# The first gate chunk of a feed-forward stage, computed before its shift is known

## The reference, cut to what matters

```python
mod = jax.nn.silu(c) @ ada_w + ada_b
sh1, sc1, g1, sh2, sc2, g2, sh3, sc3, g3 = jnp.split(mod, 9, axis=-1)
u = x * (1 + sc1[:, None, :]) + sh1[:, None, :]
y = (jax.nn.silu(u @ w_gate) * (u @ w_up)) @ w_down
x = layer_norm(ALPHA * x + 0.5 * (1 + g1[:, None, :]) * y, ln1_g, ln1_b)
...
```

## Time and profile before

| | |
|---|---|
| time, median of 3 runs | 1893.94 us (1893.53 to 1897.15) |
| span of the profiled execution | 1887.7 us (its own time beside the span is not listed; the median of the runs lies 6.2 us above the span) |
| TensorE busy | 1821.9 us, 97% of the span |
| VectorE, ScalarE, GpSimd busy | 1064.9, 817.2, 498.3 us |
| mean granted TensorE clock | 0.988 of full speed |
| chain that ended last | PE 76%, DVE 7%, POOL 7%, ACT 3%, issue 3%, DMA 3% |

### The profile page before, as it was taken

How to read it: one execution, slowest core, us unless ns; L and a number is a source line. 1 busy time by engine, 2 the same in 40 slices (tenths; PEclk the granted TensorE clock), 3 DMA queues, 4 the chain that set the end, 5 groups by cost and what they waited for, 6 DMA issues and landing times.

```text
span 1887.7 us, 22977 instructions
## 1 busy us (share of the span) xinstructions
PE 1821.9 (97%) x8904; PEld 1488.6 (79%) x8904; DVE 1064.9 (56%) x1092; ACT 817.2 (43%) x864; POOL 498.3 (26%) x644
## 2 busy tenths in 40 slices
PE   4999999999999998999999999988999999999998
PEld 3888888877887677887888888867998867888877
DVE  6565657567888896546323333368652445656452
ACT  3222223247666856227433432275222547333351
POOL 0411111032999481001000000050104996211100
PEclk8999999999999999999999999999999999999999
DMA  8566656553243133443332323354733321552411
GB/s 319 166 190 182 193 174 196 159 188 122 89 132 136 55 123 134 137 154 101 102 99 89 104 68 93 106 165 173 154 93 125 120 94 38 178 176 92 145 45 45
DMA packets 204213, 247.82 MB, mean 131 GB/s; under 512 B 5899, under 2 KB 184875, under 8 KB 202091
## 3 DMA queue, kind: packets, MB, share of 16 engines
q1 hardware_dynamic: 185643, 171.27, 28.5%
q0 software_dynamic: 13472, 51.42, 9.8%
q10 hardware_dynamic: 5024, 24.12, 3.4%
HBM read 227.39 MB, written 19.40 MB: 131 GB/s over the span
## 4 chain that ended last, share of the span: by engine, by line
PE 76%; DVE 7%; POOL 7%; ACT 3%; issue 3%; DMA 3%; SPq 1%; POOLq 0%; DVEq 0%; ACTq 0%
PE ps L2328 24%; PE ps L2131 20%; PE ps L2197 11%; POOL conv_out L488 6%; PE ps L2161 4%; PE ps L2508 2%; PE ps L2663 2%; DVE w_lo L1229 2%; PE ps L2581 2%; ACT w_hi L605 1%; DMA s_in<-u_scratch 1%; PE ps L2496 1%; DMA w_raw<-in_ffn_w_gate 1%; PE ps L2517 1%; PE ps L2563 1%
## 5 line engine op out<-in xcount | busy, mean ns | idle before, releaser
L1229 DVE TENSOR_TENSOR w_lo<-w_raw,w_hi 128x2048 fp32r<-128x2048 f32 x158 | 369.6, 2339 | 503.4 <-ACT w_hi L605 501.2
L605 ACT ACTIVATE w_hi<-w_raw 128x2048 fp32r<-128x2048 f32 x156 | 298.4, 1913 | 639.1 <-PE ps L2328 232.4
L2131 PE MATMUL ps<-u_hi,w_hi 128*128 128x512 f32 x656 | 260.1, 397 | 10.5 <-DVE w_lo L1229 10.5
L2131 PE MATMUL ps<-u_lo,w_hi 128*128 128x512 f32 x656 | 256.9, 392 | 0.0
L2131 PE MATMUL ps<-u_hi,w_lo 128*128 128x512 f32 x656 | 256.5, 391 | 0.0
L2328 PE MATMUL ps<-u_hi,w_hi 128*128 128x512 f32 x656 | 256.3, 391 | 0.0
L2328 PE MATMUL ps<-u_hi,w_lo 128*128 128x512 f32 x656 | 255.4, 389 | 0.0
L2328 PE MATMUL ps<-u_lo,w_hi 128*128 128x512 f32 x656 | 255.3, 389 | 0.0
L488 POOL TENSOR_TENSOR conv_out<-conv_out,conv_tap 128x512 f32<-128x512 f32 x120 | 194.6, 1622 | 72.0 <-ACT conv_tap L786 55.2
L2131 PEld LDWEIGHTS ps<-u_hi,w_hi 128*128 128x128 f32 x656 | 124.3, 189 | 39.4 <-DVE w_lo L1229 8.3
L2131 PEld LDWEIGHTS ps<-u_lo,w_hi 128*128 128x128 f32 x656 | 124.4, 190 | 26.1 <-issue 0.7
(11 more groups left out here) (507 smaller groups left out, 3280.8 us busy)
## 6 DMA issues: line engine op xcount, KB each, us to landing
w_raw<-in_w_in SPq DMA_DIRECT2D x44, 1024.0 KB, 5.1
ada_raw<-in_ada_w POOLq DMA_DIRECT2D x56, 512.0 KB, 4.8
w_raw<-in_ffn_w_gate SPq DMA_DIRECT2D x22, 1024.0 KB, 5.4
w_raw<-in_ffn_w_up SPq DMA_DIRECT2D x22, 1024.0 KB, 5.3
w_raw<-in_ffn_w_down SPq DMA_DIRECT2D x32, 704.0 KB, 4.5
ada_first<-in_ada_w SPq DMA_DIRECT2D x8, 1024.0 KB, 14.5
w_raw<-in_w_out SPq DMA_DIRECT2D x8, 1024.0 KB, 5.1
w_raw<-in_xa_wk SPq DMA_DIRECT2D x4, 1024.0 KB, 5.3
```

The lines of the kernel that those rows point to most:

```text
L605: A(WHI[:, slot], WRAW[:, slot], ACT.Copy).then_inc(s["w_hi"], 1)
L1229: V.tensor_tensor(WLO[:, slot], WRAW[:, slot], WHI[:, slot].bitcast(F32), ALU.subtract).then_inc(s["w_lo"], 1)
L2131: ins = M(PS[:, 2 * j + t, 0:n], w[:, j, at_:at_ + P], a[:, k, 0:n], start=(k == 0 and q == 0), stop=(k == KT - 1 and q == 2))
```

## The change

Chunk 0 (gate) is computed on x times (1 + scale) alone. The product of the weights with the shift vector, one number for each of the 256 output columns, is made by 16 products of the raw float32 weights with one column (`shift_columns`) and added as the bias of the two Silu instructions. `UH` and `UL` first hold the scaled input and are overwritten with the scaled and shifted input when chunk 0 has been computed; chunk 1 (up) is computed on that as before. The input rows are loaded ahead of the scale slices, the gate chunk ahead of the shift slices. SP loads nothing of the next pair before the small products are done, as they read the raw weights. Six of the eight rests of the scaled input are made on POOL. `lo(1, 1)` is taken into `modulate_lo`, ahead of its third k tile.

```diff
+        VF = at("x_scaled", T0, [P, 4, L])
+        SHB = at("gate_shift", S0 + 7.75, [P, 2])
@@ SP
+            sp.dma_start(XN[:], I["x"][0].rearrange("(t p) d -> p t d", p=P)).then_inc(s["x_load"], 16)
             ada_slices(0)
-            sp.dma_start(XN[:], I["x"][0].rearrange("(t p) d -> p t d", p=P)).then_inc(s["x_load"], 16)
...
+                load(0, None, 0, wk8(wg)[:, :, 0:256], True)
                 ada_slices(1)
-                load(0, None, 0, wk8(wg)[:, :, 0:256], True)
                 load(1, None, 0, wk8(wu)[:, :, 0:256], True)
                 parameter_rows()
+                sp.wait_ge(s["bias_mm"], 1)
@@ POOL, ahead of the first ada_group
+            for f in range(2, KT):
+                pool.wait_ge(s["scaled"], 2 * f + 2)
+                nc.gpsimd.tensor_tensor(UL[:, f], VF[:, f % 4], UH[:, f].bitcast(F32), ALU.subtract).then_inc(s["vl_pool"], 1)
@@ ScalarE, in ffn_act: the first pair is taken out of the loop
+                if shifted:
+                    hi_step(ph, 0, 2, 0)
+                    act.wait_ge(s["mm"], 1)
+                    act.wait_ge(s["bias_ready"], 1)
+                    act.wait_ge(s["ul_ready"], KT)
+                    A(SIL[:, 0], PS[:, 0], ACT.Silu, bias=SHB[:, 0:1])
+                    A(SIL[:, 1], PS[:, 1], ACT.Silu, bias=SHB[:, 1:2]).then_inc(s["free0"], 1)
+                    hidden(0)
+                    parameter_copies()
...
             first_hi(0)
             act.wait_ge(s["modx_ready"], 1)
+            for f in range(KT):
+                act.wait_ge(s["x_ready"], f + 1)
+                A(UH[:, f], X[:, f], ACT.Copy, scale=MODX[:, f:f + 1]).then_inc(s["scaled"], 1)
+                if f >= 4:
+                    act.wait_ge(s["vl_dve"], 2)
+                    if f >= 6:
+                        act.wait_ge(s["vl_pool"], f - 5)
+                A(VF[:, f % 4], X[:, f], ACT.Copy, scale=MODX[:, f:f + 1]).then_inc(s["scaled"], 1)
+            first_hi(1)
             act.wait_ge(s["mod_ready"], 2)
+            act.wait_ge(s["mm"], 1)
             modulate_hi(0, lambda f: MODX[:, f:f + 1], lambda f: MOD[:, SH1 + f:SH1 + f + 1])
-            first_hi(1)
@@ VectorE
             ada_first_part(0)
+            lo(0, 0)
             mod_cols(8, 16, 8)
             dve.wait_ge(s["mod_ready"], 1)
             derived(0, SC1, False).then_inc(s["modx_ready"], 1)
+            for f in range(2):
+                dve.wait_ge(s["scaled"], 2 * f + 2)
+                V.tensor_tensor(UL[:, f], VF[:, f], UH[:, f].bitcast(F32), ALU.subtract).then_inc(s["vl_dve"], 1)
             ada_first_part(1)
-            lo(0, 0)
             mod_cols(0, 8, 16)
...
-            modulate_lo(0, lambda f: MODX[:, f:f + 1], lambda f: MOD[:, SH1 + f:SH1 + f + 1])
-            lo(1, 1)
+            dve.wait_ge(s["mm"], 1)
+            dve.wait_ge(s["vl_pool"], KT - 2)
+            modulate_lo(0, lambda f: MODX[:, f:f + 1], lambda f: MOD[:, SH1 + f:SH1 + f + 1], between=lambda: lo(1, 1))
+            dve.wait_ge(s["bias_mm"], 1)
+            V.tensor_copy(SHB[:], PS[:, 6, 0:2]).then_inc(s["bias_ready"], 1)
@@ TensorE: transposes of x now ahead of mod_first(0); then
+                def part(w, a, k, j=0):
+                    for t in range(2):
+                        at_ = 256 * k + P * t
+                        ins = M(PS[:, 2 * j + t], w[:, j, at_:at_ + P], a[:, k], ...)
+                    return ins
+                def unshifted_chunk():
+                    pe.wait_ge(s["w_lo"], CB[ph] + 1)
+                    pe.wait_ge(free[0], UB[ph])
+                    for k in range(KT):
+                        if k == 6:
+                            pe.wait_ge(s["mod_ready"], 1)
+                            mod_first(1)
+                        pe.wait_ge(s["scaled"], 2 * k + 1)
+                        part(WHI, UH, k)
+                        part(WLO, UH, k)
+                        pe.wait_ge(*((s["vl_pool"], k - 1) if k >= 2 else (s["vl_dve"], k + 1)))
+                        ins = part(WHI, UL, k)
+                    ins.then_inc(s["mm"], 1)
+                def shift_columns():
+                    pe.wait_ge(s["mod_ready"], 2)
+                    for t in range(2):
+                        for k in range(KT):
+                            at_ = 256 * k + P * t
+                            ins = M(PS[:, 6, t:t + 1], WRAW[:, 0, at_:at_ + P], MOD[:, SH1 + k:SH1 + k + 1],
+                                    start=(k == 0), stop=(k == KT - 1))
+                    ins.then_inc(s["bias_mm"], 1)
+                def second_chunk():
+                    pe.wait_ge(s["w_lo"], CB[ph] + 2)
+                    pe.wait_ge(free[1], UB[ph])
+                    for k in range(KT):
+                        pe.wait_ge(s["ul_ready"], n_ul + k + 1)
+                        part(WHI, UH, k, 1)
                        part(WLO, UH, k, 1)
                        ins = part(WHI, UL, k, 1)
                    ins.then_inc(s["mm"], 1)
...
-                    first_chunk()
+                    unshifted_chunk()
+                    shift_columns()
+                    second_chunk()
                     parameter_columns()
-                    chunk(0, 1)
```

More of the change, by code:

```diff
@@ L284, in build_program @@
                  "y_mm y_gelu y_store yf_load sgs_load yh2 yl2 gsig gz gzn zh zl mem_load "
-                 "mem_ss mem_root mem_scaled mem_t mf_ready mh ml kv_store kv_load s_mm smax_ready exp_done "
-                 "s_sum p_scaled p_t pt_ready o_mm oh ol xrow_ready row_sum row_ss or_ready out_store "
-                 "consts_load dec_load0 dec_load1 s5_ranged s5_pows").split()
+                 "mem_ss mem_scaled mf_ready mh ml kv_store kv_load s_mm smax_ready exp_done "
+                 "s_sum p_scaled pt_ready o_mm oh ol xrow_ready row_sum row_ss or_ready out_store "
+                 "consts_load dec_load0 dec_load1 s5_ranged s5_pows scaled vl_dve vl_pool bias_mm bias_ready").split()
         s = {n: ctx.enter_context(nc.semaphore(n)) for n in names}
@@ L673, in first_hi, with ffn_act, hidden @@
                 A(WHI[:, slot], WRAW[:, slot], ACT.Copy).then_inc(s["w_hi"], 1)
[L675 to L680, removed]
+            def ffn_act(ph, call, shifted=False):
+                def hidden(i):
                     hi_step(ph, i, 2, 1)
@@ L685, in ffn_act @@
                     A(HH[:, bass.ds(2 * i, 2)], HF[:], ACT.Copy).then_inc(s["hid_hi"], 1)
+                if shifted:
[7 more added lines that the diff above has]
+                    parameter_copies()
+                with act.Fori(1 if shifted else 0, 11) as i:
+                    hi_step(ph, i, 2, 0)
+                    act.wait_ge(s["mm"], CB[ph] + 2 * i + 1)
+                    act.wait_ge(s["free1"], UB[ph] + i)
+                    A(SIL[:], PS[:, 0:2], ACT.Silu).then_inc(s["free0"], 1)
+                    hidden(i)
             def split_only(ph, m, its):
@@ L694, in _, with parameter_copies @@
             act.wait_ge(s["modx_ready"], 1)
+            for f in range(KT):
[7 more added lines that the diff above has]
+            first_hi(1)
             act.wait_ge(s["mod_ready"], 2)
+            act.wait_ge(s["mm"], 1)
             modulate_hi(0, lambda f: MODX[:, f:f + 1], lambda f: MOD[:, SH1 + f:SH1 + f + 1])
-            first_hi(1)
[L698 to L703, removed]
+            def parameter_copies():
+                for g in range(1, 5):
+                    act.wait_ge(s["param_t"], 5)
+                    src = PS[:, 5, g % 4 * P:g % 4 * P + PROWS[g]]
+                    A(PR[:, g * P:g * P + PROWS[g]], src, ACT.Copy).then_inc(s["param_cols"], 1)
+            ffn_act("ffn1", 0, True)
             act.wait_ge(s["lam_step"], 2)
@@ L715, in memory_act @@
                         act.wait_ge(s["mem_ss"], t + 1)
-                    A(XS[:, 15, 0:2], XS[:, 14, 0:2], ACT.Sqrt, scale=1.0 / D, bias=EPSC[:, 1:2]).then_inc(s["mem_root"], 1)
+                    A(XS[:, 15, 0:2], XS[:, 14, 0:2], ACT.Sqrt, scale=1.0 / D, bias=EPSC[:, 1:2]).then_inc(s["mem_ss"], 1)
                 if n >= 4:
                     f = n - 4
-                    act.wait_ge(s["mem_t"], f + 1)
+                    act.wait_ge(s["x_t"], KT + f + 1)
                     A(MF[:, f], PS[:, 1 + 2 * (f % 2), 0:MEM], ACT.Identity, scale=col("norm_mem_g_2", f)).then_inc(s["mf_ready"], 1)
@@ L945, in _ @@
             act.dma_start(va_dram, VAS[:]).then_inc(s["kv_store"], 16)
-            act.wait_ge(s["s5_col"], 1)
+            act.wait_ge(s["s5_act"], 1)
             A(SX[:, 0], SCOL[:, 64:96], ACT.Exp).then_inc(s["s5_act"], 1)
-            act.wait_ge(s["c_t"], 1)
+            act.wait_ge(s["s5_t"], 2)
             for t in range(2):
@@ L1163, in exps @@
                 if h >= 2:
-                    act.wait_ge(s["p_t"], h - 1)
+                    act.wait_ge(s["wt_t"], 4 + h - 1)
                 for t in range(TT):
@@ L1169, in probs_t @@
             def probs_t(h):
-                act.wait_ge(s["p_t"], h + 1)
```

(30 more changed lines are left out.)

14 lines of the change are left out of this document (6 added, 8 removed).

## The result

| | before | after |
|---|---|---|
| time, median (lowest to highest), 4 runs each | 1893.74 us (1892.77 to 1897.15) | 1902.07 us (1900.72 to 1902.65) |
| span of the profiled execution | 1887.7 us | 1898.7 us |
| first pair of chunks ends, pair 1 begins | 64.8 us | 73.1 us |

The ratio of the times is 1.0045, 95% interval 1.0034 to 1.0057: slower by 0.45%. 1903.8 was predicted, with pair 1 at 74.7.

What follows compares the result with a forecast made beforehand. VectorE's scale and shift parts, not bandwidth, were taken to hold TensorE. Chunk 0 starts 11.5 us earlier, but the late shift part, sums, products and slower clock put pair 1 at 74.7 against 64.8: +9.9, 1903.8 us, range 1895 to 1908.

Steps and rivals of the forecast that it cites:

- VectorE's two parts hold TensorE, not bandwidth: Head before the change: VectorE's scale and shift parts, each some 10.1 us of work, delay TensorE's start at 39.99.
- Pair 1 as the one number: End of the first pair of chunks: 64.8 us before, 74.7 after, 9.9 later, added to the median time.
- Shift part 31.4 to 47.6, six collisions at 1.04: VectorE's shift multiply-adds beside POOL's six subtractions: 6.2 us added, ending at 47.6 instead of 41.5.
- The row at 661 us: Trace pairing with POOL's additions used for the collisions: VectorE's 128x512 tensor_tensor goes from 0.68 to 1.72, 1.04 more.
- that at 72.76: Trace pairing beside POOL's one-input TENSOR_SCALAR: four multiply-adds take 3.69 instead of 3.11, 1.19 times.
- TensorE idle some 5 us before mod_first(1), which takes 3.54; tiles 6 and 7 in 5.2: Within chunk 0: TensorE waits for the shift part, then runs at 1.2 GHz; chunk 0 done at 56.5.
- shift_columns 5.3: Between the chunks: 16 narrow products, the middle of 7.1 and 3.5, ending at 61.8; 4.1 lost in any case.
- Chunk 1 in 12.5: After the shift products: 10.9 at full clock plus 1.6 for a restart at 1.2 GHz, ending at 74.3.
- No contention: Rival at the shift part: POOL does not slow VectorE, 6.2 less, +3.7, 1897.6 us; chance 0.08.
- Mild contention: Rival at the shift part: VectorE slows only 1.19 times, part ends at 43.2, 1899.4 us; chance 0.12.
- full exclusion: Rival at the shift part: each collision costs a whole POOL operation, 1.6 more, 1905.4 us; chance 0.08.
- The clock that holds: Rival at TensorE: wait and narrow products don't lower the clock; pair 1 at 67.7, +2.9, 1896.8 us; chance 0.12.

Runs made afterwards that it cites:

- the last of these: Changed kernel with sum in PSUM, all rests on POOL, lo(1, 1) early, 10 of 16 shift products mixed into chunk 1: pair 1 at 64.71, ratio 1.0013.
- the run without it: Changed kernel with POOL's six subtractions replaced by memsets, so POOL only writes: 1895.01 us, ratio 1.0014.

## Why the prediction was right, step by step

- *VectorE's two parts hold TensorE, not bandwidth.* Only half so. In the chain before it is the gate chunk's landing at 33.8 with its two halves that ends last, at 38.0; the shift part with mod_first(1) ends at 37.4, 0.6 ahead. The sum didn't suffer, as the change moves both and each was followed by itself.
- *Pair 1 as the one number.* Right in the main: +9.9 predicted, +8.3 there and +8.3 in the medians. That these two agree to a tenth is luck, as the interval of the ratio reaches from 6.4 to 10.8 us. In the timed runs the number holds to within 2.6 us: pair 1 at +1.6, +3.9, +5.7, 0.0, −3.1 and −0.1 went with +2.6, +2.6, +5.7, −1.7, −1.7 and +2.5 (ratios by 1892). In the last of these pair 1 stands where it stood before and the time is longer beyond its interval, so pair 1, read from one trace, does not tell the whole of it. Of the 6.2 us between span and median before, 1.9 to 2.0 lie beside the span in the runs that list both; the rest is scatter of the one profiled execution.
- *Scale ready 27.7, chunk 0 at 28.5.* 28.3 and 29.19. The gate chunk's DMA ended at 23.75, not 23.1; its two halves end last, as in the sum.
- *Shift part 31.4 to 47.6, six collisions at 1.04.* 31.53 to 46.98; six at 0.88, shown by taking POOL's reads away. The row at 661 us was the nearer one, though it gave 0.9 too much over the six; that at 72.76 was the wrong one. POOL's operation there has one input; no run tests that this is the reason. The Trainium skill (SBUF — State Buffer, Who interferes with whom) says that a VectorE instruction with two SBUF inputs contends with a GpSimd instruction that reads SBUF and not with one that only writes; both experiments agree (9.41 us for the seven beside writes alone, and 8.12 for six with one operand in PSUM). The same section of the Trainium skill calls the contention an exclusive lock, and speaks of a block for the whole instruction where VectorE uses both of its ports. Read as a block for a whole POOL instruction it would have cost an estimated 6 x 1.30 = 7.8; 5.26 was measured, so the measurement decides for less.
- *TensorE idle some 5 us before mod_first(1), which takes 3.54; tiles 6 and 7 in 5.2.* 6.16, 3.54 and 5.34, at a clock of 0.50.
- *shift_columns 5.3.* The term furthest off: 3.89, or 0.12 a pass. The clock rose just as the products began (0.91 in 56 to 58), so they ran near the lower end of the two that I gave, and lo(1, 1), which I had as a floor 4.1 behind chunk 0, became the gate: 60.10 for 61.8. Between the chunks 4.1 passed for 5.3, which is 1.2 of the 1.6 by which pair 1 came earlier than predicted; the rest is chunk 0's end at 56.01 for 56.5, mostly from the smaller collisions. The middle of two ends was a choice without a row.
- *Chunk 1 in 12.5.* 12.62, with 0.50 in 60 to 62. The 1.6 for the restart was chosen between its bounds, and so close a hit is luck: the other runs took up to 13.9. The row for the fall, at 1370 us, is no clean case either: behind the 16-column products stand products of 64 columns and a wait of 0.68 us.
- *Weights of pair 1 covered, 3.3 to spare.* The gate's half was ready at 69.9, 3.2 ahead.
- *Rivals.* No contention would have been 1897.6; the run without it gave 1.0014, some 1896.4 on 1893.74. Mild contention would make a multiply-add 1.6 (1.19 x 1.34) and full exclusion 2.6 (1.34 + 1.30); 2.11 to 2.27 lies between, next to the forecast's 2.3. The clock that holds was refuted by the stretches at 0.50, and in part by the run with mod_first(1) last: the products pay what it saves. Not asked at all was what x first gives; the sum was right since both landings were taken from rows, but the reason was unseen until it was undone.

## What to carry to other kernels

Starting the large engine earlier gains nothing while the input that it needs half-way is made later by the same edit: follow the late input to its engine and ask what the newly early work does to that engine. Before two engines' work is laid side by side, look where their operands lie; moving a running sum to PSUM took the whole collision away here. Where two gates end within half a us of each other, an experiment on one alone shows nothing: take both away.

## What the runs showed of the hardware that was not expected

- Narrow float32 products (128x128 weights, one column) took 0.11 to 0.13 us a pass at 2.4 GHz and 0.22 at 1.2 GHz. The same 32 passes took 3.9 to 4.4 us behind wide matmuls and 7.0 behind other narrow ones.
- Spreading them among wide matmuls did not keep the clock: 0.50 from 48 to 54 us with TensorE busy throughout, and pair 1 3.0 us later (0.5 of it from before) than with the same products in one block.
- VectorE's scaling of 128x1024 from SBUF took 0.75 into SBUF and 1.28 into PSUM, while the two-operand multiply-add took 1.28 to 1.30 either way.
